# Last MLP chunk as seven block products, weight sums on VectorE, their low parts on GpSimd

## The reference

```python
def channel_mixer(x, g_norm, w1, w2):
    h = rms_norm(x, g_norm)
    return x + jnp.square(jax.nn.relu(h @ w1)) @ w2

for layer in range(DEPTH):          # DEPTH = 2
    x = even_layer(x, ...) if layer % 2 == 0 else odd_layer(x, ...)
    x = channel_mixer(x, ff_g_norm[layer], ff_w1[layer], ff_w2[layer])
```

## Time and profile before

| what | value |
| --- | --- |
| median of 3 runs | 2167.59 us (2167.36 to 2168.07) |
| span of the profiled execution, first to last instruction | 2164.5 us |
| PE busy | 2130.0 us (98%) |
| DVE busy | 1245.9 us (58%) |
| POOL busy | 1171.0 us (54%) |
| ACT busy | 845.1 us (39%) |
| mean granted TensorE clock | 0.998 |

### The profile page before, as it was taken

One profiled execution on the slowest core, in us unless ns is written; L12 is line 12 of the kernel. 1 busy time (PEld: TensorE's weight loads), 2 busy tenths in 40 slices (PEclk: granted clock), 3 DMA queues, 4 the chain that ended last, 5 costly groups with the idle time before them and its releaser, 6 DMA issues.

```text
span 2164.5 us, 31199 instructions
## 1 busy us (share of the span) xinstructions
PE 2130.0 (98%) x10042; PEld 1779.3 (82%) x10042; DVE 1245.9 (58%) x2045; ACT 845.1 (39%) x1290; POOL 1171.0 (54%) x700
## 2 busy tenths in 40 slices
PE   7999899999999999999999999999999999999999
PEld 6887788888888998888888888888888888888887
DVE  6697758888887436377777244367777443111111
ACT  6554564232333653342322334532332443232331
POOL 6865744564654005564655646754655664554653
PEclk9999999999999999999999999999999999999999
DMA  6321112332332103323323232333333333333332
GB/s 212 98 69 50 69 47 72 108 97 90 105 98 78 52 11 99 98 90 104 97 88 107 88 98 78 108 97 98 98 98 98 89 97 127 107 97 98 98 96 90
DMA packets 58545, 199.93 MB, mean 92 GB/s; under 512 B 6704, under 2 KB 6960, under 8 KB 58416
## 3 DMA queue, kind: packets, MB, share of 16 engines
q1 hardware_dynamic: 58272, 198.19, 29.4%
q10 hardware_dynamic: 144, 0.02, 0.0%
HBM read 193.99 MB, written 4.19 MB: 92 GB/s over the span
## 4 chain that ended last, share of the span: by engine, by line
PE 89%; DVE 2%; issue 1%; ACT 1%; POOL 0%; DVEq 0%; ACTq 0%; POOLq 0%
PE psum L630 27%; PE psum L632 27%; PE psum L631 27%; PE psum L805 2%; PE psum L654 2%; PE psum L781 1%; PE psum L782 1%; PE psum L712 0%; PE psum L643 0%; PE psum L637 0%; DVE small L1721 0%; DVE small L1541 0%; PE psum L722 0%; ACT pt_buf L1289 0%; DVE score L1726 0%
## 5 line engine op out<-in xcount | busy, mean ns | idle before, releaser
L973 POOL TENSOR_TENSOR w_buf<-raw,w_buf 128x1024 fp32r<-128x1024 f32 x334 | 812.2, 2433 | 579.2 <-ACT w_buf L1283 568.2
L1283 ACT ACTIVATE w_buf<-raw 128x1024 fp32r<-128x1024 f32 x320 | 337.0, 1053 | 486.6 <-PE psum L632 450.2
L630 PE MATMUL psum<-hid_buf,w_buf 128*128 128x512 f32 x1344 | 525.9, 391 | 0.0
L632 PE MATMUL psum<-hid_buf,w_buf 128*128 128x512 f32 x1344 | 523.3, 389 | 0.0
L631 PE MATMUL psum<-hid_buf,w_buf 128*128 128x512 f32 x1344 | 523.1, 389 | 0.0
L630 PE MATMUL psum<-h_buf,w_buf 128*128 128x512 f32 x1216 | 475.1, 391 | 0.0
L632 PE MATMUL psum<-h_buf,w_buf 128*128 128x512 f32 x1216 | 473.2, 389 | 0.0
L631 PE MATMUL psum<-h_buf,w_buf 128*128 128x512 f32 x1216 | 473.1, 389 | 0.0
L1904 DVE SCALAR_TENSOR_TENSOR psum<-y_buf,wdw,psum 128x512 f32<-128x512 f32 x464 | 314.0, 749 | 0.0
L1883 DVE TENSOR_TENSOR xt<-xt,psum 128x512 f32 (+1 forms) x160 | 109.9, 687 | 331.1 <-PE psum L632 331.0
L631 PEld LDWEIGHTS psum<-hid_buf,w_buf 128*128 128x128 f32 x1344 | 252.5, 188 | 52.8 <-issue 1.0
(11 more groups left out here) (255 smaller groups left out, 2113.4 us busy)
## 6 DMA issues: line engine op xcount, KB each, us to landing
raw<-weights SPq DMA_DIRECT2D x348, 512.0 KB, 3.5
xt<-x_t SPq DMA_DIRECT2D x2, 2048.0 KB, 8.6
x_in<-x_t SPq DMA_DIRECT2D x12, 256.0 KB, 7.0
early<-weights SPq DMA_DIRECT2D x4, 512.0 KB, 7.7
out_t<-xt SPq DMA_DIRECT2D x1, 2048.0 KB, 9.4
out_t<-xt SPq DMA_DIRECT2D x8, 256.0 KB, 2.0
b_tok<-x_t SPq DMA_DIRECT2D x4, 256.0 KB, 5.8
ws<-w_s SPq DMA_DIRECT2D x1, 512.0 KB, 7.3
```

What stands on the lines that cost most here:

```text
L630: nc.tensor.matmul(acc, lhs_hi, rhs_hi, start=first, stop=False)
L632: return nc.tensor.matmul(acc, lhs_lo, rhs_hi, start=False, stop=last)
L973: nc.gpsimd.tensor_tensor(dst_lo, src, dst_hi.bitcast(F32), ALU.subtract).then_inc(done, 1)
L1283: nc.scalar.activation(w_buf[:, 0, :, slot * P:(slot + 1) * P], raw[:, slot % 2], ACT.Copy).then_inc(hi_up, 1)
```

## The change

The fourth chunk (`q = 3`) of `ff1` is taken out of both halves (`SOLO = 3`) and done at the end for both halves together (`PAIRED`). The chunk is a product of a weight matrix of 1024 x 1024 with activations of 1024 x 1024 tokens (both halves side by side), once up and once down. Each of the two is cut into 2 x 2 blocks of 512, and made with seven block products in place of eight. The seven are named by their weight operand, in this order: A11, A12, S2 (a sum of three weight blocks), S3 (a difference of two), A22, S1 (a sum of two), S4 (a difference of two). Their activation operands are blocks or sums of blocks of the same kind. A block product is 4 steps `g`, each one output tile: 4 contraction tiles x 3 matmuls = 12 matmuls. So there are 2 x 28 = 56 steps in the paired part. `v` counts block products, 0 to 13.

The work around a step:

- SP loads tiles of 512 x 128 (256 KB, 8 slots) in place of blocks of 512 KB, 88 in all.
- DVE sums the weight tiles of S2 (two instructions a step), S3, S1 and S4 (one), seven steps ahead (`sum_weights(g + 7)`).
- ACT makes high parts of weights and POOL the low parts, five steps ahead, 128x512 each.
- DVE sums the activation blocks of the next block product (`sum_activations`), ACT makes their high parts and DVE their low parts (`low_activations`). PE waits for these (`b_lo`) ahead of each of the four contraction tiles of a block product's first step.
- DVE reads the bank of every step: `read_hidden` in the up part (with the partial sums between the blocks, a relu and the norm's factor), `read_output` in the down part.

Around it: the unscaled activations of both halves are kept (`h_first`, `h_second`). `xt0` is stored to DRAM as of the start of `ff1` of half 0 and loaded again (2 MB each way), and `match_first` brings half 0 to the norm factors of half 1, with ten DVE instructions behind the first up units of `ff1` of half 1. Since `ff1` of half 0 is one chunk shorter, the 248 taps of half 1 start earlier: 32 in `pw1` of half 1, 28 in `pw2` of half 0, and 188 in the two first chunks of `ff1` of half 0. The output of half 0 is stored in the last part of the kernel rather than under `ff1` of half 1.

```diff
-          ("pw2", 0, PW2, 8), ("ff1", 0, FF1, 64), ("pw2", 1, PW2, 8), ("ff1", 1, FF1, 64)]
+          ("pw2", 0, PW2, 8), ("ff1", 0, FF1, 16 * SOLO), ("pw2", 1, PW2, 8), ("ff1", 1, FF1, 16 * SOLO)]
...
+READS = {A11: ((0, 0),), A12: ((0, 1),), S2: ((1, 0), (1, 1), (0, 0)), S3: ((0, 0), (1, 0)), A22: ((1, 1),),
+         S1: ((1, 0), (1, 1)), S4: ((0, 1),)}
+SUMS = {S2: 2, S3: 1, S1: 1, S4: 1}
+B_SUMS = {S2: 2, S3: 1, A22: 1, S1: 1}
...
# PE
+            for g in range(PAIRED_STEPS):
+                v, term, p = g // 4, term_of(g), g % 4
+                pe.wait_ge(w_lo, g + 1)
+                if before_in_bank(g) >= 0:
+                    pe.wait_ge(product_read, before_in_bank(g) + 1)
...
+                for j in range(4):
+                    if v >= 2 and p == 0:
+                        pe.wait_ge(b_lo, b_lo_count(v, j))
...
+                    nc.tensor.matmul(acc, hi, h_buf[:, 0, k, :], start=start, stop=False, skip_group_check=True)
+                    nc.tensor.matmul(acc, hi, h_buf[:, 1, k, :], start=False, stop=False, skip_group_check=True)
+                    mm = nc.tensor.matmul(acc, lo, h_buf[:, 0, k, :], start=False, stop=j == 3, skip_group_check=True)
+                mm.then_inc(product_up, 1)
...
# POOL
+            for at in range(-SUM_AHEAD, PAIRED_STEPS):
+                g = at + SPLIT_AHEAD
+                if 0 <= g < PAIRED_STEPS:
+                    rows, cols = w_slot(g)
+                    pool.wait_ge(w_hi, g + 1)
+                    T(w_buf[:, 1, rows, cols], w_source(g), w_buf[:, 0, rows, cols].bitcast(F32), ALU.subtract
+                      ).then_inc(w_lo, 1)
...
# DVE
+            def low_activations(v, j):
+                dve.wait_ge(b_hi, b_lo_count(v, j))
+                at = b_at(v, j)
+                V.tensor_tensor(h_buf[:, 1, at, :], b_source(v, j), h_buf[:, 0, at, :].bitcast(F32), ALU.subtract
+                                ).then_inc(b_lo, 1)
...
+            def read_hidden(g):
...
+                dve.wait_ge(product_read, g - {A12: 4, S1: 8, S4: 16}[term] + 1)
+                V.tensor_tensor(x, bank, x, ALU.add).then_inc(product_read, 1)
+                dve.wait_ge(product_read, g + 1)
+                V.scalar_tensor_tensor(out=x, in0=x, scalar=0.0, in1=rms_bc[:], op0=ALU.max, op1=ALU.mult
+                                       ).then_inc(pair_relu, 1)
...
+                if term == S2:
+                    if g >= STAGE_STEPS:
+                        dve.wait_ge(w_summed, done)
+                    V.tensor_tensor(dst, tiles[0], tiles[1], ALU.add).then_inc(w_summed, 1)
+                    dve.wait_ge(w_summed, done + 1)
+                    V.tensor_tensor(dst, dst, tiles[2], ALU.subtract).then_inc(w_summed, 1)
...
+            for g in range(PAIRED_STEPS):
+                if g + SUM_AHEAD < PAIRED_STEPS:
+                    sum_weights(g + SUM_AHEAD)
+                v, p = g // 4 + 1, g % 4
+                if v >= 2 and 4 * v < PAIRED_STEPS:
+                    if p < 2 and v % TERMS in B_SUMS:
+                        sum_activations(v, (2 * p, 2 * p + 1))
+                    if p >= 2:
+                        low_activations(v, 2 * p - 4)
+                        low_activations(v, 2 * p - 3)
+                dve.wait_ge(product_up, g + 1)
+                (read_output if g // STAGE_STEPS % 2 else read_hidden)(g)
```

More of the change, by code:

```diff
@@ L60 @@
 EARLY = (2, 3, 6, 7)
+SOLO = 3
 NBLOCK = ZB + 160
@@ new lines, in _ @@
+                if (name, half) == ("ff1", 1):
+                    stream(first, first_block, 0, 8)
+                    sp.wait_ge(x_saved, 16)
+                    sp.wait_ge(act_in, 2 * KT)
+                    sp.dma_start(h_first[:], x_kept[:]).then_inc(h_first_in, 16)
+                    stream(first, first_block, 8, count)
+                    continue
+                stream(first, first_block, 0, count)
+            for n, (g, block_index, late) in enumerate(W_TILES):
+                at = n % W_SLOTS
+                if n < 4:
+                    sp.wait_ge(lo_up, 32 + NUNIT)
+                elif n < W_SLOTS:
+                    sp.wait_ge(hid_lo, CREDIT + HIDDEN)
+                else:
+                    user = W_TILES[n - W_SLOTS][0]
+                    if term_of(user) in SUMS:
+                        sp.wait_ge(w_summed, sums_through(user))
+                    else:
+                        sp.wait_ge(w_lo, user + 1)
+                sp.dma_start(w_tile[at], weights[block_index][:, 4 * late:4 * late + 4, :]).then_inc(w_tile_in[at], 16)
@@ L626, in _ @@
+            last = PAIRED_STEPS - STAGE_STEPS
+            for term, row, half in ((A12, 0, 1), (A22, 4, 1), (S1, 4, 0), (S4, 0, 0)):
+                for p in range(4):
+                    sp.wait_ge(product_read, last + 4 * term + p + 1)
+                    sp.dma_start(out_t[row + p, :, half * HALF:(half + 1) * HALF], xt[half][:, row + p]
+                                 ).then_inc(out_sem, 16)
+            sp.wait_ge(out_sem, 16 * 2 * KT)
         @block.tensor
@@ L916, in mlp @@
                         units(first + 16 * q, 8, operand)
-                    late = q == 3 and (stage, half) == ("ff1", 0)
+                    late = q == SOLO - 1 and (stage, half) == ("ff1", 0)
                     down = first + 16 * q + 8
@@ L1470, in mlp, with keep_second @@
                                    swish(1, hid_buf) if (stage, half) == ("ff1", 0) else None)
-                    units(first + 16 * q + 8, 8, job, last=(q == 3 and (stage, half) == ("ff1", 1)))
+                    units(first + 16 * q + 8, 8, job, last=(q == SOLO - 1 and (stage, half) == ("ff1", 1)))
+            def keep_second(i, r):
+                k = 4 * i + r
+                nc.scalar.activation(h_second[:, k, :], flat(xt[1], None, k), ACT.Copy, scale=gflat(G_FF1, k)
+                                     ).then_inc(h_second_up, 1)
             for name, half, _, count in STAGES:
@@ L1494, in _ @@
                 elif name == "pw2":
-                    units(first, 8, final(first, half, f"ff1_{half}", G_FF1, OPERAND[name, half][1]))
+                    prepare = final(first, half, f"ff1_{half}", G_FF1, OPERAND[name, half][1])
+                    units(first, 8, both(prepare, keep_second if half else None))
                 elif name == "pw1":
@@ L1923, in swish_arg, with match_first @@
                 return job
+            def match_first():
+                dve.wait_ge(h_first_in, 16)
+                link(V.reciprocal(conv_bc[:], rms_bc[:]))
+                link(V.tensor_tensor(rms_kept[:], rms_kept[:], conv_bc[:], ALU.mult))
+                for k in range(KT):
+                    V.scalar_tensor_tensor(out=h_first[:, k, :], in0=h_first[:, k, :], scalar=gflat(G_FF1, k),
+                                           in1=rms_kept[:], op0=ALU.mult, op1=ALU.mult).then_inc(h_first_up, 1)
             def mlp(stage, half, following):
@@ L1956, in mlp @@
                     late = (stage, half) == ("ff1", 0)
-                    if conv and q < 3:
+                    if conv and q < (SOLO - 1 if late else 3):
                         for r in range(16):
@@ L2052, in _, with sum_activations @@
                     mlp(name, half, {("ff0", 1): ("pw1_1", G_OD, hid_buf)}.get((name, half)))
+            def sum_activations(v, tiles):
+                n, term = v // TERMS, v % TERMS
+                b11, b12, b21, b22 = (b_block(n, row, col) for row in range(2) for col in range(2))
+                if term == S2:
+                    if n % 2:
+                        dve.wait_ge(pair_square, 16 * (n // 2) + 12 + tiles[-1] + 1)
+                    else:
+                        dve.wait_ge(h_first_up, KT)
+                        dve.wait_ge(h_second_up, KT)
+                    for j in tiles:
+                        V.tensor_tensor(b_kept[:, j, :], b22(j), b12(j), ALU.subtract).then_inc(b_sum, 1)
+                    for j in tiles:
+                        dve.wait_ge(b_sum, b_summed(v, j) - 2)
+                        V.tensor_tensor(b_kept[:, j, :], b_kept[:, j, :], b11(j), ALU.add).then_inc(b_sum, 1)
+                    return
+                dve.wait_ge(product_up, 4 * (v - 1))
+                for j in tiles:
+                    left, right = {S3: (b22, b12), A22: (b21, lambda j: b_kept[:, j, :]), S1: (b12, b11)}[term]
+                    V.tensor_tensor(b_source(v, j), left(j), right(j), ALU.subtract).then_inc(b_sum, 1)
```

240 lines of the change are left out of this document (217 added, 23 removed).

## The result

The changed kernel takes 2172.78 us (median of six runs, 2172.22 to 2174.77), the kernel before 2166.97 (six runs, 2166.46 to 2168.07). The medians lie 5.8 us apart. The ratio is 1.0028, 95% interval 1.0017 to 1.0039: slower, by 0.28%. The span of the profiled execution is 2170.6 us, 6.1 more than before, with 96 matmuls fewer. In what follows, "lost" in the paired part is its length from the start of PE's first matmul to 0.23 us after the start of its last, less the 152.3 us of 56 steps without a stall. A block product has 48 matmuls and takes 10.88 us without one. A figure of what is lost is read from one traced execution of a version, a time is a median of several.

A forecast was written before the change was run, and what follows sets the result against it. PE's matmuls bound the kernel. The change wins 21.8 us of PE work but loses 26.8 to DVE's lateness (28.8 less 2): span 2164.5 to 2169.5, plus 3.1 to the median, 2172.6 us; range 2156 to 2187.

The forecast's parts named there:

- the clock: PE's granted clock falling under 1.0 behind stalls, named only as a way to be wrong; no size given.
- What is removed: Four sets of 8 units, 174.1 us, give way to 56 steps, 152.3 us; PE's work falls by 21.8 us.
- POOL mostly hidden: Rival: POOL lies beside DVE's reads and waits as far as it can; 10.9 us late, 2156.7 us; chance 0.17.
- never hidden: Rival: POOL never lies beside anything, 4.6 us in each window, 42.9 us late, 2188.7 us; chance 0.10.
- forecast over: DVE's queue per four-step window, with POOL's share, beyond the 10.88 us of a block product; 28.8 us in all.
- less 2: DVE may be about 2 us late once before PE waits for low parts; taken off the 28.8 us.
- Eight slots ahead and a late DVE cover it: Weight tiles at S2: three wanted a step, 289 GB/s for four steps, costed at nothing.
- The largest single stall: PE's wait at step 8, ahead of S2, some 8 us.
- POOL's toll in steps 4 to 7: POOL's exclusion of DVE in that window: 3.4 us on top of DVE's own 17.5.
- The three signs of being wrong: PE standing still for weight tiles, for the taps, or the granted clock falling under 1.0 behind the stalls.
- Until the paired part nothing should shift by more than 1 us.: Everything ahead of the paired part was to keep its time within 1 us.
- The taps: Convolution taps beside `pw1` and `pw2` units, 3.9 and 4.6 us of DVE against 5.44 a unit; no cost.

The follow-up runs named there:

- the version of all three: Changed kernel with fewer taps at the end of `pw1`, the up part's activation sums made early, and DVE's order inside a step interleaved: 2158.72 us, 0.996.
- the last version: Changed kernel with early up-part activation sums, DVE's interleaved order, and 24 `pw1` taps, none beside the first two units: 2156.28 us, 0.9955.

## Why the prediction was right

The forecast was 2172.6 us and 2172.78 were measured; 26.8 lost were forecast and 25.6 found. So near a hit is partly luck. The span came out 1.1 us over the forecast of 2169.5, and median and span lay 2.2 apart in place of 3.1. The 3.1 was itself chance: every timed execution on record is 1.7 to 1.9 us over its own span, and the trace of the kernel before was a quick one. More of the luck lies in the sum, below: it had more waits than were found, and no term for the clock.

**What is removed.** 56 steps at 2.72 and the removal of 32 units hold. Block products without a stall take 10.88 us, and the balance of the spans, 6.1, is within 0.1 of the 25.6 lost, less 21.8, plus the 1.7 at `pw2` and the 0.5 by which this execution was later before it (a copy of DVE at 1340.15 stood at 1339.58 in the kernel before).

**DVE's own work against POOL's part.** The working gives DVE alone 6.6 + 0.7 + 2.2 - 2 = 7.5 and POOL the other 19.3. With POOL's instructions narrowed 6.1 stayed and 19.5 went, the latter with what the clock adds. This is the step on which the sign hung, and the run shows it: the same DVE work without POOL beside it is 13 us faster than the kernel before. The rival "POOL mostly hidden" (2156.7) was to win if under about 60% of the POOL time that was counted met DVE. In the eight windows that write this time out it is 24.4 us, and there the instructions with two SBUF inputs took 20.5 us more than 0.68 each, 84%. The rival "never hidden" (2188.7) fell as well: it has 4.6 in each of eleven windows, 50.6, and 29.9 were found.

**Where the stalls stand.** What DVE has over in one window shows at the first step of the next block product, as a wait of PE ahead of it or ahead of its third contraction tile. Laid to the windows in this way, the 25.5 us are:

| steps | forecast over | lost |
| --- | --- | --- |
| 4 to 7 | 10.0, less 2 | 8.9 |
| 8 to 11 | 0.1 | 0 |
| 12 to 15 | 1.5 | 1.4 |
| 16 to 27 | 3.6 + 1.5 + 0.8 | 1.5 + 0 + 0 |
| 28 to 31 | 1.7 | 3.8 |
| 32 to 35 | 5.8 | 6.6 |
| 36 to 39 | 0.1 | 0 |
| 40 to 47 | 1.5 + 2.2 | 1.4 + 1.9 |

Steps 16 to 27 were priced too high. Steps 28 to 31 came out too low: "Eight slots ahead and a late DVE cover it" didn't hold for the tile of 2086.54, for which DVE idled 2.88 us in that very window. No run takes that wait alone away. At step 8 the 8.9 for 8.0 is not the right price either. The wait ahead of it is 3.9 and the one ahead of the third contraction tile 1.5; the other 3.5 are matmuls at the lower clock. The largest single stall was to be some 8 us and was 3.9. POOL's toll in steps 4 to 7 was priced at 3.4, and the instructions there ran 1.8 us long, since their eight activation sums all took 0.68 or 0.69.

**What was named as a sign.** The paired part lasts 177.9 us (175 to 185 forecast), DVE is 92% busy in its first half (near 90%), tensor_tensor instructions with two SBUF inputs average 0.91 us (0.85 or more), the chain runs through L2356. The three signs of being wrong came too, each of them small beside 25.6: DVE waited for tiles (4.3 us), PE stood still for the taps' sake (1.7), and the clock fell.

**A step that failed.** "Until the paired part nothing should shift by more than 1 us." The taps were costed at nothing, unit by unit. What was overlooked is that the convolution's first taps stand ahead of an operand that POOL needs at a moment when POOL has next to no slack behind it. It cost 1.7 us.

**A term that was missing.** The clock. The prediction named it only as a thing that could go wrong. In the stretch behind the largest stall:

```profile
2015.00:2025.00 10.00, 8.85 (x23) 6.56 (x23) 9.93 (x14) 5.05 (x10) 5.25 (x4) 0.56 0.48 157
```

The granted clock is 0.56 there, so most of the stretch is at the lower of the two levels (1.2 GHz, 0.5 of full speed), after a stall of 4.15 us from start to start, and the matmuls at 2015.57 and 2016.00 stand 0.43 us apart in place of 0.23. Over the paired part the spacings of 0.25 to 0.5 us come to 5.4 us more than at 0.23. They lie within the 25.6. The eleven spacings over 0.6, PE's waits, come to 18.1 (1.8 more lie in between the two), where the forecast had 26.8 of waits alone. But not all of the 5.4 is owed to the clock: DVE catches up while PE is slow, and would have made PE wait for some of it. How much was not settled. The clock fell a second time around step 36: from 2106 to 2109 it is 0.50, behind a spacing of 2.58 us and one of 0.94. With the stalls of at most 1.8 us that POOL narrowed leaves, such spacings cost 0.5, in the version of all three 1.6, in the last one 2.5.

## What to carry to other kernels

When matmuls are traded for sums on DVE, price a two-SBUF-input instruction with what GpSimd does in the same step, not by its duration alone: here 0.68 us became 0.92 in the mean, from no change for some groups to 1.16 for the low parts, and with the clock that was 19 of the 26 us lost. Sum DVE's queue over the period after which PE needs its results (a block product here) and look for the windows that are over, then move work out of just those windows: the 20 sums of the up part, made as 16 in a stage where DVE was idle, were worth 11 us of 2172.8. Move all of them: eight sums that took 6.9 us from the largest stall made the whole only 5.3 shorter.

## What the hardware showed unexpectedly

The prediction assumed that a POOL instruction shuts DVE out whenever it begins. The traces show two cases. In one, instructions of DVE with two SBUF inputs, back to back, go ahead of a POOL instruction that has already begun. POOL gets in at DVE's next instruction with an operand in PSUM, and the following exclusive instruction pays. In the last version, DVE:

```profile
2085.85 0.68 DVE L2435 TENSOR_TENSOR w_kept_b<-w_kept_b,w_more 128x512 f32<-128x512 f32 x1
2086.45 1.28 DVE L2364 TENSOR_TENSOR pair_hid<-pair_hid 128x512 f32<-128x512 f32 x2
2087.66 1.28 DVE L2367 TENSOR_TENSOR b_kept<-pair_hid 128x512 f32<-128x512 f32 x2
2088.86 0.67 DVE L2415 TENSOR_TENSOR xt<-xt,psum 128x512 f32<-128x512 f32 x1
2089.46 1.16 DVE L2440 TENSOR_TENSOR w_sum<-raw 128x512 f32<-128x512 f32 x1
```

and POOL:

```profile
2086.05 4.02 POOL L1358 TENSOR_TENSOR w_buf<-w_kept_a,w_buf 128x512 fp32r<-128x512 f32 x1 [5.48 <-ACT w_buf L1741]
```

POOL begins at 2086.05 and ends at 2090.07. Its usual 1.30 counted back from there is 2088.77, the start of DVE's read of PSUM, while four exclusive instructions between took no longer than 0.68. The version of all three with the taps at their first place shows the same (POOL 4.01 us from 2089.61, DVE's read at 2092.41), and so does the changed kernel (POOL 3.44 us from 2099.47, DVE's read at 2101.67). In the first stall above POOL's 1.83 from 2011.28 reaches over the read at 2011.90.

In the other case POOL gets in between two such instructions, though they are as close. The rows are from the changed kernel. The first of DVE's two takes 0.68 us and the second 1.78; two that aren't disturbed take 1.29 together:

```profile
2035.12 2.38 DVE L2351 TENSOR_TENSOR b_f<-h_second,b_kept 128x512 f32<-128x512 f32 x2
...
2035.33 1.63 POOL L1351 TENSOR_TENSOR w_buf<-w_more,w_buf 128x512 fp32r<-128x512 f32 x1 [2.48 <-ACT w_buf L1734]
```

This is the more frequent one. Ten times in the paired part of the changed kernel a POOL instruction begins under an undelayed DVE instruction with two SBUF inputs that has another such right behind it. Seven times the next one takes 1.76 to 1.79 us, three times it takes 0.68 or 0.69. What decides between the two isn't settled here. POOL's spans are rough, the DVE rows are what the reading rests on.

The Trainium skill (SBUF — State Buffer, Who interferes with whom) says that whoever issues first holds the shared pair for the whole instruction and that issue order decides who blocks. The trace agrees that the two exclude each other. It doesn't agree that the one whose instruction began first always goes first: four DVE instructions that began after POOL's went ahead of it.
